# Expert weights in transfers of two chunks, another order of the last scatter, and the few-rows body last in its loop

## What is computed

```python
scores = sigmoid(x @ w_router)                 # (256, 16)
# the best of 4 groups per token, its 2 best experts, gates normalised
for e in range(16):
    h = silu(x @ w_gate[e]) * (x @ w_up[e])    # (256, 1024)
    y = y + combine[..., e:e+1] * (h @ w_down[e])
```

## Time and profile before

| | us |
|---|---|
| median of 3 runs | 1501.25 (1498.96 to 1503.79) |
| the profiled execution | 1501.84 |
| its span, first to last instruction | 1499.9 |
| PE busy | 1292.3 (86%) |
| DVE busy | 430.3 (29%) |
| mean granted clock of PE | 0.94 |

### The profile page before, as it was taken

The page is one execution under the profiler, slowest core; times in us unless marked ns, Lnnn a source line. Parts: engine busy times, 40 slices in busy tenths (PEclk is TensorE's granted clock), DMA queues, the critical chain, the costliest instruction groups (busy, mean ns, idle before and its releaser), DMA issues.

```text
span 1499.9 us, 19495 instructions
## 1 busy us (share of the span) xinstructions
PE 1292.3 (86%) x7884; PEld 535.9 (36%) x7885; DVE 430.3 (29%) x811; ACT 147.9 (10%) x255; POOL 76.0 (5%) x138
## 2 busy tenths in 40 slices
PE   3899999899999999789989989988768778777866
PEld 2555544455445564323323323322212222221221
DVE  3212695777566340201111110121111111110112
ACT  3000101244101033000000000000000000000000
POOL 0112100111222000000000000000000000000000
PEclk9999999999999999999999989989889988978987
DMA  9999668566888759999999999999999999999996
GB/s 375 420 392 411 251 257 338 200 223 238 309 337 320 267 220 422 419 419 421 422 421 422 421 422 422 421 420 422 421 422 422 421 422 422 422 422 421 423 420 249
DMA packets 84355, 559.43 MB, mean 373 GB/s; under 512 B 9680, under 2 KB 9680, under 8 KB 22608
## 3 DMA queue, kind: packets, MB, share of 16 engines
q1 hardware_dynamic: 69408, 502.49, 81.6%
q0 software_dynamic: 14320, 52.01, 9.3%
q10 hardware_dynamic: 576, 4.19, 0.7%
HBM read 556.57 MB, written 2.10 MB: 372 GB/s over the span
## 4 chain that ended last, share of the span: by engine, by line
PE 51%; DMA 41%; DVE 3%; issue 2%; ACT 1%; SPq 1%; DVEq 0%; ACTq 0%
DMA ring<-w_gate_dram 17%; DMA ring<-w_up_dram 15%; PE ps L845 8%; PE ps L840 7%; PE ps L675 7%; PE ps L572 7%; DMA rope_heads<-w_down_dram 3%; PE ps L872 3%; DMA ring<-w_in_dram 3%; PE ps L566 3%; PE ps L866 2%; PE ps L813 2%; PE ps L577 2%; PE ps L801 2%; DMA big<-ctx_dram 1%
## 5 line engine op out<-in xcount | busy, mean ns | idle before, releaser
L840 PE MATMUL ps<-ring,early 128*32 128x256 f32 x2304 | 174.9, 442 | 62.0 <-DMA ring<-w_gate_dram 30.9
L845 PE MATMUL ps<-ring,early 128*64 128x512 f32 x672 | 168.6, 628 | 25.1 <-DMA ring<-w_gate_dram 16.5
L1545 DVE TENSOR_TENSOR big<-ps,big 128x1024 f32<-128x1024 f32 x64 | 75.4, 1219 | 312.1 <-PE ps L801 312.1
L572 PE MATMUL ps<-ring,big 128*128 128x512 f32 x320 | 146.5, 600 | 0.0
L840 PEld LDWEIGHTS ps<-ring,early 128*32 128x32 f32 x2304 | 71.7, 121 | 176.5 <-DMA ring<-w_gate_dram 59.0
L1170 DVE SCALAR_TENSOR_TENSOR halves<-ring,silu_c,halves 128x1024 f32<-128x1024 f32 x96 | 123.1, 1283 | 40.5 <-DMA ring<-w_half_dram 33.9
L675 PE MATMUL ps<-ring,big 128*128 128x512 f32 x256 | 112.2, 594 | 1.3 <-ACT big L1055 1.3
L845 PEld LDWEIGHTS ps<-ring,early 128*64 128x64 f32 x672 | 43.0, 142 | 134.7 <-issue 69.1
L572 PEld LDWEIGHTS ps<-ring,big 128*128 128x128 f32 x320 | 59.2, 192 | 69.6 <-issue 69.4
L675 PEld LDWEIGHTS ps<-ring,big 128*128 128x128 f32 x256 | 47.9, 190 | 58.4 <-issue 58.4
L801 PE MATMUL ps<-halves,early 64*128 64x512 f32 x256 | 65.9, 634 | 0.0
(11 more groups left out here) (330 smaller groups left out, 1065.1 us busy)
## 6 DMA issues: line engine op xcount, KB each, us to landing
ring<-w_gate_dram SPq DMA_DIRECT2D x128, 1024.0 KB, 25.7
ring<-w_up_dram SPq DMA_DIRECT2D x64, 1024.0 KB, 26.0
ring<-w_down_dram SPq DMA_DIRECT2D x64, 1024.0 KB, 26.2
ring<-w_half_dram POOLq DMA_DIRECT2D x96, 512.0 KB, 6.5
ring<-w_mix_dram SPq DMA_DIRECT2D x32, 1024.0 KB, 12.0
big<-w_up_dram SPq DMA_DIRECT2D x32, 1024.0 KB, 26.3
big<-w_down_dram SPq DMA_DIRECT2D x32, 1024.0 KB, 23.9
ring<-w_in_dram SPq DMA_DIRECT2D x28, 1024.0 KB, 9.2
```

The costliest lines, as they stand in the source:

```text
L572: mm = pe.matmul(ps[:, b + t, :], nT[:, k, t * P:(t + 1) * P], w, start=(k == 0), stop=(k == KT - 1))
L840: mm = pe.matmul(out_b[0][BASE * f:BASE * (f + 1), :], rows[0][:, k, :], w[:, kk, f * 256:(f + 1) * 256], start=(k == 0), stop=(k == KT - 1))
L845: mm = pe.matmul(out_b[1][REST * f:REST * (f + 1), :], rows[1][:, k, :], w[:, kk, f * N:(f + 1) * N], start=(k == 0), stop=(k == KT - 1))
L1545: tt(y, banks[:, 2 * h:2 * h + 2, :].rearrange("p a n -> p (a n)"), y, ALU.add).then_inc(done, 1)
```

## The change

Four things, and one that goes with them:

- Two chunks make one transfer of 2 MiB, with 16 KB on each partition: the weights lie in memory as [4, 128, 4096] for each matrix, the 12 slots become 6 pairs of neighbours (`param` and `rope_heads` become one tile `late` for it), and SP issues 12 transfers a job. A pair waits until both of its slots have been used. PE waits once for each pair. Chunks 10 and 11 of job 0 wait together for the candidates.
- The last scatter does, in a first turn, half 0 of tile 0 and half 1 of tile 1, and in a second turn the other two; the adds and the stores follow in that order. Its waits stand ahead of all its matmuls.
- In the loop over the rest, the branch is turned round, so that the few-rows body stands last.
- A many-rows or middle job scatters the few-rows job before it without the matmuls of the rest block (`ahead=(0,)`).

```diff
-        job_slots = [ring[:, i, :] for i in (6, 7, 0, 1, 2, 3, 4, 5)]
-        job_slots += [big[:, MORE:MORE + CH], big[:, MORE + CH:MORE + 2 * CH], param[:, 0:CH], rope_heads[:]]
+        job_pairs = [ring[:, i:i + 2, :].rearrange("p s n -> p (s n)") for i in (6, 0, 2, 4)]
+        job_pairs += [big[:, MORE:MORE + 2 * CH], late[:, 0:2 * CH]]
...
+        last_banks = [Yb, ps[:, 0:4, :]]
+        last_order = ((0, 0), (1, 1), (1, 0), (0, 1))
...
-            for i in range(JCH):
+            for i in range(JPAIR):
                 if i == 0:
                     sp.wait_ge(half_step, HALF_SLOTS + 6 * KT)
-                elif i == 8:
+                elif i == 4:
                     sp.wait_ge(logit_done, 1)
-                elif i == 10:
-                    sp.wait_ge(mask_ready, 1)
-                elif i == 11:
+                elif i == 5:
                     sp.wait_ge(cand_ready, 1)
...
+                if i < 4:
+                    sp.wait_ge(slot_free, used_job(2 * i + 1 - SLOTS))
+                elif i >= PAIR_SLOTS:
+                    sp.wait_ge(slot_free, used_job(2 * i + 1 - JOB_SLOTS))
+                sp.dma_start(job_pairs[i % PAIR_SLOTS], weights[i // 4][FIRST_EXPERT, i % 4]) \
+                    .then_inc(job_landed[i % PAIR_SLOTS], 16)
...
+                for i in range(JPAIR):
+                    sp.wait_ge(slot_free, j * JCH + used_job(2 * i + 1 - JOB_SLOTS))
+                    w = weights[i // 4][bass.ds(e, 1)].rearrange("e i p n -> (e i p) n")
+                    sp.dma_start(job_pairs[i % PAIR_SLOTS], w[(i % 4) * P:(i % 4 + 1) * P, :]) \
+                        .then_inc(job_landed[i % PAIR_SLOTS], 16)
...
-                with pe.If(few):
-                    experts(j, (0,), first)
-                with pe.Else():
-                    with pe.If(some):
-                        experts(j, (1,), first)
+                    with pe.If(few * -1 + 1):
+                        with pe.If(some):
+                            experts(j, (1,))
+                        with pe.Else():
+                            experts(j, (0, 1))
                     with pe.Else():
-                        experts(j, (0, 1), first)
+                        experts(j, (0,))
...
-                    experts(i * 2 + 2, (0, 1))
+                    experts(i * 2 + 2, (0, 1), ahead=(0,))
...
-                    experts(i * 2 + 2, (1,))
+                    experts(i * 2 + 2, (1,), ahead=(0,))
...
-            scatter(jobs, 0)
-            scatter(jobs, 1, ps[:, 0:4, :])
+            pe.wait_ge(outs_saved[0], jobs)
+            pe.wait_ge(outs_saved[1], jobs)
+            pe.wait_ge(spread_saved, jobs)
+            pe.wait_ge(summed, jobs * 4)
+            for turn in range(2):
+                for q in range(4):
+                    t = (q // 2 + turn) % 2
+                    pe.matmul(last_banks[t][:, q, :], spread_T[0][BASE * q:BASE * (q + 1), t, :],
+                              outs[0][BASE * q:BASE * (q + 1), :], start=True, stop=True)
+                for q in (0, 2, 1, 3):
+                    t = (q // 2 + turn) % 2
+                    mm = pe.matmul(last_banks[t][:, q, :], spread_T[1][REST * (q // 2):REST * (q // 2 + 1), t, :],
+                                   outs[1][REST * (q // 2):REST * (q // 2 + 1), q % 2, :], start=False, stop=True,
+                                   skip_group_check=True)
+                    if q % 2:
+                        mm.then_inc(scattered, 1)
...
-            add_rows(jobs, 0, out_ready)
-            add_rows(jobs, 1, out_ready, ps[:, 0:4, :])
+            for i, (t, h) in enumerate(last_order):
+                dve.wait_ge(scattered, jobs * 4 + (i + 1))
+                y = tokens[:, t, h * 1024:(h + 1) * 1024]
+                tt(y, last_banks[t][:, 2 * h:2 * h + 2, :].rearrange("p a n -> p (a n)"), y, ALU.add) \
+                    .then_inc(out_ready, 1)
```

More of the change, by code:

```diff
@@ L41 @@
 JOB_SLOTS = 12
+JPAIR, PAIR_SLOTS = JCH // 2, JOB_SLOTS // 2
 FIRST_EXPERT = NE - 1
@@ L189, in build @@
         const = sb("const", [P, CONST_COLS])
-        param = sb("param", [P, PARAMS])
+        late = sb("late", [P, CH + PARAMS])
+        rope_heads, param = late[:, 0:CH], late[:, CH:]
         big = sb("big", [P, 2 * TT * D + KT * 2 * SEQ + P])
@@ L312, in build @@
         landed = [sem(f"landed{i}") for i in range(SLOTS)]
-        job_landed = [sem(f"job_landed{i}") for i in range(JOB_SLOTS)]
+        job_landed = [sem(f"job_landed{i}") for i in range(JOB_SLOTS // 2)]
         slot_free = sem("slot_free")
@@ L416, in _ @@
                 e = sp.value_load(n_i[0:1, bass.ds(j, 1)], min_val=0, max_val=NE - 1)
[L417 to L422, removed]
+                for i in range(JPAIR):
[3 more added lines that the diff above has]
+                        .then_inc(job_landed[i % PAIR_SLOTS], 16)
+            for q, (t, h) in enumerate(last_order):
                 sp.wait_ge(out_ready, q + 1)
-                t, h = q // 2, q % 2
                 sp.dma_start(out[t * P:(t + 1) * P, h * 1024:(h + 1) * 1024],
@@ L785, in table, with scatter @@
                 mm.then_inc(table_done, 1)
-            def scatter(j, t, banks=Yb):
+            def scatter(j, t, parts=(0, 1)):
                 if t == 0:
@@ L793, in scatter @@
                 for q in range(4):
-                    if t == 1 and q % 2 == 0 and banks is Yb:
+                    if t == 1 and q % 2 == 0:
                         pe.wait_ge(summed, j * 4 + (1 + q // 2))
-                    pe.matmul(banks[:, q, :], spread_T[0][BASE * q:BASE * (q + 1), t, :],
-                              outs[0][BASE * q:BASE * (q + 1), :], start=True, stop=True)
-                if t == 0:
+                    mm = pe.matmul(Yb[:, q, :], spread_T[0][BASE * q:BASE * (q + 1), t, :],
+                                   outs[0][BASE * q:BASE * (q + 1), :], start=True, stop=True)
+                    if q % 2 and 1 not in parts:
+                        mm.then_inc(scattered, 1)
+                if t == 0 and 1 in parts:
                     pe.wait_ge(outs_saved[1], j)
-                for q in (0, 2, 1, 3):
-                    mm = pe.matmul(banks[:, q, :], spread_T[1][REST * (q // 2):REST * (q // 2 + 1), t, :],
+                for q in (0, 2, 1, 3) if 1 in parts else ():
+                    mm = pe.matmul(Yb[:, q, :], spread_T[1][REST * (q // 2):REST * (q // 2 + 1), t, :],
                                    outs[1][REST * (q // 2):REST * (q // 2 + 1), q % 2, :], start=False, stop=True,
@@ L815, in sort_rows, with experts @@
                     mm.then_inc(sort_done, 1)
-            def experts(j, parts, first=False):
+            def experts(j, parts, first=False, ahead=(0, 1)):
                 def arrived(i):
-                    pe.wait_ge(job_landed[i % JOB_SLOTS], j * (16 * JCH // JOB_SLOTS) + 16 * (i // JOB_SLOTS + 1))
-                    return job_slots[i % JOB_SLOTS]
+                    p = i // 2
+                    if i % 2 == 0:
+                        pe.wait_ge(job_landed[p % PAIR_SLOTS],
+                                   j * (16 * JPAIR // PAIR_SLOTS) + 16 * (p // PAIR_SLOTS + 1))
+                    return job_pairs[p % PAIR_SLOTS][:, i % 2 * CH:(i % 2 + 1) * CH]
                 rows = [xg[:, :, REST:BLK] if 1 in parts else xg[:, :, 0:BASE], xg[:, :, 0:REST]]
@@ L831, in experts @@
                     elif m == 1:
-                        scatter(j, 0)
+                        scatter(j, 0, parts=ahead)
                     for i in range(8):
@@ L850, in experts @@
                 else:
-                    scatter(j, 1)
+                    scatter(j, 1, parts=ahead)
                 pe.wait_ge(hidden_ready, j + 1)
@@ L878, in any_job @@
                 if first:
-                    few, some = first_few, first_some
+                    with pe.If(first_few):
+                        experts(j, (0,), first)
+                    with pe.Else():
+                        with pe.If(first_some):
+                            experts(j, (1,), first)
+                        with pe.Else():
+                            experts(j, (0, 1), first)
                 else:
@@ L1559, in hidden_product @@
                 else:
-                    add_rows(j, 1, summed)
+                    add_rows(j, 1)
                 dve.wait_ge(ehT_done, j + 1)
```

20 lines of the change are left out of this document (8 added, 12 removed).

## The result

The changed kernel takes 1489.57 us in the median of 8 runs (1484.34 to 1493.66), the kernel before 1501.55 in 8 (1497.47 to 1506.28): a ratio of 0.9918, interval 0.9894 to 0.9942, 12.0 us faster.

What follows compares the result with a forecast made beforehand. It took the full DMA stream, from 551.4 us to the last landing, as the bound. Rate -16.7, start +0.9, tail +1.7 and code -1.0 sum to -15.1: from 1501.8 to 1486.7 us, range 1482 to 1504.

Steps and rivals of the forecast that it cites:

- the likeliest case: Whole kernel: the summed terms hold, giving 1486.7 us, own range 1482 to 1492; chance 0.64.
- Rate: Weight stream: 16 KB rows halve the packets, 10 ns each, raising the rate to 429.5 GB/s over 186 pairs: -16.7 us.
- 9 fewer on each of 16 engines: Weight stream: a pair takes 144 packets, not 288, completion ones included, saving 90 ns of 4975 a pair.
- The chance of 0.13: Rival on the weight stream: a smaller gain, from a fixed packet cost well below 10 ns; chance 0.13.
- Holes: Weight stream in the jobs: coarser slots leave no pause, as left-out matmuls give 3.9 us back: 0.
- 2.1 us stay ahead: End of a many-rows job: work still queued ahead of a pair's issue after all gains and losses, so no hole.
- nearly 2 us are left: Shallowest issue, at 598 us: queued work ahead falls from 2.8 us to nearly 2, so no hole.
- the third rival, the dry queue: End of many-rows jobs: some 4 us hole in each of 3; with no rate gain, 1515 us; together chance 0.05.
- Start: Start of the unbroken stream, 551.4 us: chunks 12 and 13 wait for both slots, one consumed chunk later: +0.9 us.
- Second chunk behind the landing: Tail: PE has two chunks, not one, left after the last landing: +1.7 us, or +0.9 at the higher clock.
- Code ahead of the scatter: Before the last scatter: with the few-rows body last, PE jumps over no bodies: -1.0 us, bounds 0 and -1.3.
- The scatter's turns: Last scatter: two halves complete per turn as before, so 0; the clock may move it 1.6 us either way.

Runs made afterwards that it cites:

- e12: The changed kernel with the few-rows body back at the head of the loop over the rest, run once more: one run, 1488.0 us.
- e6: The changed kernel with the rest-block matmuls back in the scatters of the many-rows and middle jobs: ratio 0.9975 to the kernel before.
- e7: The changed kernel with the few-rows body back at the head of the loop over the rest: ratio 0.9925 to the kernel before.
- e3: The rest alone: the kernel before with scatter order, branch order and left-out matmuls changed, transfers still of one chunk: ratio 0.9978 to the kernel before.
- e11: The kernel called the pairs alone, run once more: one run, 1497.6 us.
- the pairs alone: The changed kernel with scatter order, branch order and many-rows jobs' scatters put back, leaving only the two-chunk transfers: ratio 0.9960 to the kernel before.
- e10: The changed kernel with 4 MiB transfers, rows of 32 KB and three slots of four chunks: ratio 1.0138 to the kernel before.
- e5: The changed kernel with each pair as two 1 MiB transfers on 64 partitions each, rows of 16 KB: median 2037 us for 1503.

## Why the prediction was right

The forecast was 1486.7 us; the median is 1489.6, inside the likeliest case's own range, and the case came as described: a higher rate by longer rows, with the left-out matmuls keeping the queue filled. Term by term:

- **Rate, -16.7 forecast.** Right in kind: rows of 16 KB are single packets, and the row is what counts (8 KB rows in 2 MiB transfers gain nothing). Mis-sized: a is 9.5 ns and not 10, and only data packets have it, so a pair saves 8 x 9.5 = 76 ns (4.972 - 4.896) and not 90; 186 x 0.076 is 14.1 us. The step that overcounted is "9 fewer on each of 16 engines": completion packets cost nothing that shows, as 2 MiB transfers with 8 KB rows had it. The chance of 0.13, the smaller gain of the forecast's numbers, was the author's for a fixed cost well below 10 ns; no run shows one, the traces have 9.5 ns at rows of 8, 16 and 32 KB. The instruction queue's slow 16 KB packets meant nothing for the data queue, where one took 0.62 us: they are slow by themselves, 0.94 us for one with nothing else moving (before, 1487.6 to 1488.6 us: 1 packet, 5.9% of 16 engines). Following the full streams was the right choice.
- **Holes, 0 forecast.** Right in the balance, wrong at its edges. The left-out matmuls were to give back what the coarse slots take; without them 6 to 7 us of stream are lost, the forecast having some 2 in each of 3 jobs. But "2.1 us stay ahead" holds for the mean alone: 3.6, 2.2 and 0.3 were left in jobs 2, 4 and 6, and 3.8, 0.2 and 1.7 in e12. And "nearly 2 us are left" at 598 us was about right as a number (the pair landed 9.0 us after its issue, 1.5 over an idle queue) and wrong as a reason for no dip: the slice fell to 246 GB/s. A margin of 1.5 us did not keep the stream full. So of the signs named, "no slice below 400" did not hold in slices of 2 us, and the sign of the third rival, the dry queue, came, a dip at the end of job 6, but a small one (408 GB/s in its slice). Both places together are the difference between 186 x 0.076 = 14.1 and the 12.5 (11.2 to 12.5 in four profiles) that the stream gained: 1.6 to 2.9 us, for the rival's 12.
- **Start, +0.9 forecast.** Too small to be seen: the start scatters over 9 us.
- **Second chunk behind the landing, +1.7 forecast.** 3.32 us for two at a granted clock of 0.56, 1.70 for one before at 0.64: +1.6. At a granted 1.00 two took 1.97 (e6, e7) and one 1.11 (e3), the +0.9 that the forecast put beside it.
- **Code ahead of the scatter, -1.0 forecast.** The profile showed -1.1, which is an execution and not a law: the same program with the old order shows 1.19 and 0.18. What was not foreseen is the other side, 12 us of issue at the head of job 15; that the DMA leads there held.
- **The scatter's turns, 0.** Two halves complete in each turn as before, at the same 3.06 us where the granted clock is 1.00. The 1.6 us that the first profile gains are the clock (1.00 in the first turn, for 0.63 in the earlier trace rows), named as a bound: this turn took 3.06 us in 8 of the 12 profiles with coarser slots and 4.6 to 4.9 in the other 4, and 4.6 to 4.7 in both with single chunks. That matmuls without a pause ahead of it bring the rise is not shown: 3.32 us of them stood before a turn at 1.00 (after), 3.69 before one at 0.64 (e11).

The stream gains 11.2 to 12.5; the tail is 16.0, 16.0, 16.1 and 17.4 in the profiles of the changed kernel and of the two with the sort later, for 17.1 in the only one before, where the forecast had +0.7; and the medians say 12.0. Part of how near the forecast came is luck: the rate and the holes together fell short by 4.2 to 5.5 us, and the clock in the tail made some of it good. The last landing, at 1466.4 us for the 1467 named, came there only by the early start; once more it was at 1473.8.

The two halves of the change are worth little apart and more together, and this is the holes: the pairs alone take 4.2 to 5.7 us off the stream, the rest alone nothing, both 11.2 to 12.5. The ratios by themselves (0.40% and 0.22% apart, 0.82 to 0.89% together) would not tell it, as the sum of 0.62% lies within the intervals of both runs of the whole.

## What to carry to other kernels

Where a stream of weights is the bound, count its packets: here a contiguous run of memory for each partition was one packet at 8, 16 and 32 KB, each cost 9.5 ns of its engine beside 36.8 us for every MB, and 2 MiB in place of 1 gave nothing at the same row (422 GB/s in both). Make the rows longer in memory, but price the coarser slots with it: take the issue-to-landing time at the shallowest issue, less that of an idle queue, and compare it with the time in which the consumer frees one more chunk; 1.5 us left gave a dip here, 3.6 none. Work that is off the path under fine slots, such as matmuls on zero rows, may be what keeps the queue filled under coarse ones: here 6 to 7 us of the stream hung on them, and nothing with single chunks (932.0 us for 931.4).

## What the runs showed of the hardware that was not expected

- Transfers to 64 of the 128 partitions ran at 223 GB/s for 428, with the 16 engines at a share of 100.4% and each packet at about twice its time (1.18 us for 0.62), though the transfer for the other half was queued behind. What halves it was not tried.
- Rows of 32 KB stay single packets: 2638 data packets for 86.44 MB (32.8 KB each) at 432 GB/s, 1% over the 428 of 16 KB.
- PE stood for 11.4 to 13.8 us without a matmul where a branch leads it past two bodies that it doesn't run (seven profiles, e10 the least, e5 the most), 5.6 to 5.9 with the body first (two profiles), at the same place of the same loop. Two kernels with the body last had less: 5.94 with the rest-block matmuls back, 8.86 in the rest alone. That it is code loading is a reading of the row, and was not tried by itself.
- The same program had 1.19 and 0.18 us of such a stall ahead of its last scatter in two executions.
